# First modulation pieces as rows on TensorE, sums between the input transposes, and idle products in TensorE's waits

## What is computed

```python
c_act = silu(c)                                  # one row of 1,024
mod = c_act @ ada_w[layer] + ada_b[layer]        # 1,024 x 6,144 weights
sh_m, sc_m, g_m, sh_f, sc_f, g_f = split(mod, 6)
h = rms_norm(x, pre_mix_g) * (1 + sc_m) + sh_m   # the first normed input
u, v = split(gelu(h @ w_in + b_in), 2)           # the first large product
```

## Time and profile before

| | |
|---|---|
| median of 3 runs | 2,061.39 us (2,058.17 to 2,063.58) |
| the profiled execution's own time | 2,065.57 us |
| its span, first to last instruction | 2,063.9 us |
| mean granted TensorE clock | 0.980 |
| TensorE busy | 95% of the span |
| VectorE, ScalarE, GpSimd busy | 38%, 35%, 49% |

### The profile page before, as it was taken

How to read it: one execution, slowest core, us unless ns; L and a number is a source line. 1 busy time by engine, 2 the same in 40 slices (tenths; PEclk the granted TensorE clock), 3 DMA queues, 4 the chain that set the end, 5 groups by cost and what they waited for, 6 DMA issues and landing times. The chain is left out here.

```text
span 2063.9 us, 28068 instructions
## 1 busy us (share of the span) xinstructions
PE 1964.4 (95%) x10804; PEld 1680.5 (81%) x10804; DVE 792.3 (38%) x1382; ACT 717.5 (35%) x1153; POOL 1001.9 (49%) x541
## 2 busy tenths in 40 slices
PE   5999999999999989998998999999999999989997
PEld 5998888888888878877878888888777997857997
DVE  5666533444444046343634111010327750036212
ACT  2324325322221254343635222222534233335333
POOL 1635644466665434546633655544433443624642
PEclk9999999999999999999999999999999999998999
DMA  7655453556656313232112333322222334311232
GB/s 261 201 164 164 163 171 105 153 173 189 189 169 207 97 56 95 72 102 82 52 42 67 99 100 93 100 92 99 76 74 72 92 93 109 78 41 32 66 99 82
DMA packets 220323, 230.68 MB, mean 112 GB/s; under 512 B 15456, under 2 KB 185224, under 8 KB 219960
## 3 DMA queue, kind: packets, MB, share of 16 engines
q1 hardware_dynamic: 215392, 213.28, 34.3%
q10 hardware_dynamic: 4824, 15.88, 2.3%
HBM read 226.33 MB, written 2.79 MB: 111 GB/s over the span
## 5 line engine op out<-in xcount | busy, mean ns | idle before, releaser
L742 POOL TENSOR_TENSOR w_lo<-raw,w_hi 128x1024 fp32r<-128x1024 f32 (+1 forms) x296 | 732.2, 2488 | 577.8 <-ACT w_hi L735 577.6
L1391 PE MATMUL acc<-hh,w_hi 128*128 128x512 f32 (+1 forms) x1472 | 558.4, 379 | 18.8 <-DVE hl L2029 9.4
L1391 PE MATMUL acc<-hh,w_lo 128*128 128x512 f32 (+1 forms) x1472 | 549.5, 373 | 0.0
L1391 PE MATMUL acc<-hl,w_hi 128*128 128x512 f32 (+1 forms) x1472 | 549.2, 373 | 0.0
L735 ACT ACTIVATE w_hi<-raw 128x1024 fp32r<-128x1024 f32 (+1 forms) x296 | 308.3, 1051 | 396.8 <-DMA raw<-in_ffn_w_down 152.5
L1391 PEld LDWEIGHTS acc<-hh,w_hi 128*128 128x128 f32 x1472 | 280.8, 191 | 77.5 <-issue 17.4
L1391 PEld LDWEIGHTS acc<-hl,w_hi 128*128 128x128 f32 x1472 | 281.1, 191 | 48.1 <-issue 1.7
L1391 PEld LDWEIGHTS acc<-hh,w_lo 128*128 128x128 f32 x1472 | 280.5, 191 | 48.4
L1391 PE MATMUL acc<-w_hi,hh 128*128 128x256 f32 x704 | 203.3, 289 | 3.3 <-POOL hl L1272 3.3
L1391 PE MATMUL acc<-w_hi,hl 128*128 128x256 f32 x704 | 200.8, 285 | 0.0
L1391 PE MATMUL acc<-w_lo,hh 128*128 128x256 f32 x704 | 200.8, 285 | 0.0
(11 more groups left out here) (502 smaller groups left out, 2902.2 us busy)
## 6 DMA issues: line engine op xcount, KB each, us to landing
raw<-in_ffn_w_gu SPq DMA_DIRECT2D x176, 256.0 KB, 3.3
raw<-in_w_in SPq DMA_DIRECT2D x52, 512.0 KB, 3.6
ada_raw<-in_ada_w SPq DMA_DIRECT2D x50, 512.0 KB, 3.9
raw<-in_ffn_w_down SPq DMA_DIRECT2D x44, 512.0 KB, 3.6
raw<-in_a_w_in SPq DMA_DIRECT2D x32, 512.0 KB, 3.7
ada_raw<-in_ada_w ACTq DMA_DIRECT2D x30, 512.0 KB, 5.7
raw<-in_a_w_out SPq DMA_DIRECT2D x16, 512.0 KB, 3.6
ada_raw<-in_kv_ada_w SPq DMA_DIRECT2D x16, 512.0 KB, 5.4
```

Of the source, the lines that this page charges most:

```text
L742: eng.tensor_tensor(w_lo[:, s, part, :], raw[:, s, part, :], w_hi[:, s, part, :].bitcast(F32), ALU.subtract).then_inc(w_split, 1)
L1391: ins = pe.matmul(out, w, x, start=first and n == 0, stop=last and n == len(pairs) - 1, skip_group_check=check)
```

## The change

The first 2,048 modulation columns are cut into eight other pieces of 1 MB: 512 rows by 512 columns, named (column group, half of the rows). Three of them, (0,0), (0,1) and (1,0), go to TensorE, now with one column of `c_act` stationary and 512 columns of weights moving, so that the result is a row on one partition (`row_unit`); ScalarE copies the row, and `row_columns` turns it into four columns by products with a single one. The other five go to VectorE, four steps of 512 columns each, sums of one column group in one buffer; for (1,1) its sum joins TensorE's row. The sums over partitions move into the sequence of transposes: column group 2 ahead of the second row piece, group 1's row ahead of the third chunk, group 3 ahead of the sixth. Each VectorE step is followed by a drain. The inverse deviations and the diagonal follow the second VectorE piece and the parameter copies. Loads are in the new order, with VectorE's last piece between the first two weight units. ScalarE takes its root table ahead of the wait for `x` and splits the first two weight units after the first and second copy of `x`. Last, ten products of the identity with itself are issued at four points of TensorE's order: in both attentions between the first scores and the first transposes, in the last head's values ahead of its waits, and ahead of the waits before the sparse attention. Their result is read by nobody. Constants and semaphore numbers follow; the pieces' buffers and the wide columns' counts change by name only.

```diff
@@ -52,10 +52,12 @@
 KU = 4
 RING = 4
 REL_BUCKETS, REL_MAX_DIST = 32, 128
-ADA_PE = 2
+ADA_PE = ((0, 0), (0, 1), (1, 0))
+ADA_DVE = ((2, 0), (2, 1), (1, 1), (3, 0), (3, 1))
+ADA_HALF = 512
 ADA_SETUP = 8
-ADA_PAIRS = ADA_SETUP - 2
 ADA_WIDE = 1024
+WARM = 10
 ADA_WIDES = 12
 ADA_SLOTS = 48
...
@@ -582,6 +587,11 @@
             def last(n):
                 copy(n - 1)
             attention_loop(act, a, first, step, last)
+
+        def warm_products(pe, dst):
+
+            for _ in range(WARM):
+                pe.matmul(dst, ident[:], ident[:], start=True, stop=True)
 
...
@@ -626,6 +636,8 @@
                 pe.wait_ge(s, value)
             scores(0, 0)
             scores(0, 1)
+            pe.wait_ge(a["pt_dve"], 1)
+            warm_products(pe, aux[:, 0, 0:P])
             transposes(0)
...
@@ -765,22 +777,28 @@
         @block.sync
         def _(sp):
             sp.dma_start(c_row[:], io["c"][0].rearrange("(k p) -> k p", p=P)).then_inc(c_in, 16)
-            def whole_step(dst, s, landed_sem):
-                sp.dma_start(dst, ada_w[0][:, COLS * s:COLS * (s + 1)].rearrange("(k p) n -> p k n", p=P)).then_inc(landed_sem, 16)
-            def next_step(s):
-                whole_step(ada_next[:, s], ADA_PE + s, ada_next_in[s])
-            next_step(0)
-            whole_step(ada_first[:, 0], 0, ada_first_in[0])
-            next_step(1)
+            def ada_unit(dst, unit, landed_sem):
+                wide, half = unit
+                rows_k = ada_w[0][4 * P * half:4 * P * (half + 1), ADA_HALF * wide:ADA_HALF * (wide + 1)]
+                sp.dma_start(dst, rows_k.rearrange("(k p) n -> p k n", p=P)).then_inc(landed_sem, 16)
+            def pe_unit(s):
+                ada_unit(ada_unit_home(s), ADA_PE[s], ada_first_in[s])
+            def dve_unit(s):
+                ada_unit(ada_next[:, 1 + s], ADA_DVE[s], ada_next_in[s])
+            dve_unit(0)
+            pe_unit(0)
+            dve_unit(1)
             sp.dma_start(x_tok[:], io["x"][0].rearrange("(b p) d -> p b d", p=P)).then_inc(x_landed, 16)
-            for s in range(1, ADA_PE):
-                whole_step(ada_first[:, s], s, ada_first_in[s])
+            pe_unit(1)
             sp.wait_ge(x_landed, 16)
-            for s in range(2, ADA_SETUP - ADA_PE):
-                next_step(s)
-            load_group(sp, "mlp_v", 0, 0)
+            dve_unit(2)
+            pe_unit(2)
+            dve_unit(3)
+            load_unit(sp, S["mlp_v"], src_of["mlp_v"], 0, 0, 0)
+            dve_unit(4)
+            load_unit(sp, S["mlp_v"], src_of["mlp_v"], 0, 0, 1)
             load_group(sp, "mlp_v", 0, 1)
-            sp.wait_ge(ada_ready, ADA_SETUP - ADA_PAIRS)
+            sp.wait_ge(ada_setup_ready, 3)
...
@@ -993,14 +1011,19 @@
                     act.wait_ge(t_ready, c + 1)
                     act.activation(hi[:, k, :], tmp[:, c % 4, :], ACT.Copy).then_inc(h_hi, 1)
 
+            act.activation(warm[:], eps[:], ACT.Sqrt)
             act.wait_ge(x_landed, 16)
             for b in range(NB):
                 block_squares(b)
             act.activation(small[:, 0:NB], square_sum[:, 4, :], ACT.Sqrt, bias=eps[:], scale=1.0 / D).then_inc(std_ready, 1)
+            for wide, src in enumerate((ada_ps, bank(1))):
+                act.wait_ge(row_ps, wide + 1)
+                act.activation(ada_first[0:1, wide, 0, :], src[0:1, :], ACT.Copy).then_inc(row_sb, 1)
             for k in range(DC):
                 act.wait_ge(xt_ps, k + 1)
                 act.activation(x_first[:, k, :], XT_BANKS[k % len(XT_BANKS)], ACT.Copy).then_inc(kept_ready, 1)
-            split_hi(act, S["mlp_v"], 0, 0)
+                if k < 2:
+                    split_hi(act, S["mlp_v"], 0, 0, slice(k, k + 1))
...
@@ -1573,9 +1592,19 @@
                         wide_columns(slot // 4 - 1)
                 return before_chunk
 
-            def column_sums(dst, src):
-                for m in range(2):
-                    ins = pe.matmul(dst[:, m:m + 1], src[:, m * P:(m + 1) * P], ones[:, 0:1], start=True, stop=True)
+            def row_columns(wide):
+
+                pe.wait_ge(row_sb, wide + 1)
+                for m in range(4):
+                    pe.matmul(bank(0)[:, 4 * wide + m:4 * wide + m + 1], ada_first[0:1, wide, 0, m * P:(m + 1) * P], ones[0:1, 0:1],
+                              start=True, stop=True)
+
+            def setup_sums(wide, at):
+
+                pe.wait_ge(ada_setup_ready, at)
+                for m in range(4):
+                    ins = pe.matmul(bank(0)[:, 4 * wide + m:4 * wide + m + 1], ada_setup[:, wide - 1, m * P:(m + 1) * P], ones[:, 0:1],
+                                    start=True, stop=True)
                 return ins
...
@@ -1591,6 +1620,10 @@
                 for k in range(DC):
                     if k >= len(XT_BANKS):
                         pe.wait_ge(kept_ready, k - len(XT_BANKS) + 1)
+                    if k == 2:
+                        row_columns(1)
+                    if k == 5:
+                        setup_sums(3, 3).then_inc(ada_first_ps, 1)
                     for b in range(NB):
...
@@ -1602,23 +1635,27 @@
             pe.transpose(aux[:, 0, 0:DC], c_row[:], ident[0:DC, 0:DC]).then_inc(c_ps, 1)
 
             pe.wait_ge(c_ok, 1)
-            for s in range(ADA_PE):
+            def row_unit(s, dst):
+
+                wide, half = ADA_PE[s]
                 pe.wait_ge(ada_first_in[s], 16)
-                for m in range(2):
-                    for k in range(DC):
-                        pe.matmul(bank(0)[:, 2 * s + m:2 * s + m + 1], ada_first[:, s, k, m * P:(m + 1) * P], c_act[:, k:k + 1],
-                                  start=k == 0, stop=k == DC - 1)
+                for k in range(KU):
+                    ins = pe.matmul(dst, c_act[:, KU * half + k:KU * half + k + 1], ada_unit_home(s)[:, k, :],
+                                    start=half == 0 and k == 0, stop=half == 1 and k == KU - 1)
+                return ins
+
+            row_unit(0, ada_ps[0:1, :])
             pe.wait_ge(par_in, 16 * 19)
             for n, r in enumerate((112, 104, 74)):
                 pe.transpose(bank(1 + n)[:, 0:r], rows[0:r, n, :], ident[0:r, 0:r]).then_inc(par_t, 1)
+            setup_sums(2, 1)
+            row_unit(1, ada_ps[0:1, :]).then_inc(row_ps, 1)
             pe.wait_ge(par_ok, 3)
+            row_unit(2, bank(1)[0:1, :])
+            pe.wait_ge(ada_setup_ready, 2)
+            pe.matmul(bank(1)[0:1, :], ones[:, 0:1], ada_setup[:, 0, :], start=False, stop=True).then_inc(row_ps, 1)
+            row_columns(0)
             first_to_features()
-            for s in range(ADA_PE, ADA_PAIRS):
-                pe.wait_ge(ada_setup_ready, s - ADA_PE + 1)
-                ins = column_sums(bank(0)[:, 2 * s:2 * s + 2], ada_setup[:, s - ADA_PE, :])
-            ins.then_inc(ada_first_ps, 1)
-            for s in range(ADA_PAIRS, ADA_SETUP):
-                ada_column(s, s % 2)
...
@@ -1818,6 +1855,8 @@
 
             def head_values(h, e):
                 pe.wait_ge(m_s_ready, h + 2)
+                if h == MH - 1:
+                    warm_products(pe, ms[:, 0:P])
                 pe.wait_ge(hm_ready, h + 1)
...
@@ -1898,24 +1938,24 @@
 
             def wide_finish(q):
 
-                dve.wait_ge(ada_sum, ADA_SETUP - ADA_PAIRS + q + 1)
+                dve.wait_ge(ada_sum, q + 1)
                 cols = slice(2 * ADA_SETUP + DC * q, 2 * ADA_SETUP + DC * (q + 1))
                 dve.tensor_tensor(mod[:, cols], ada_ps[:, 0:DC], par_a[:, cols], ALU.add).then_inc(ada_col, 1)
 
-            def ada_chunks(total, w, k0):
-                for kk in range(w.shape[1]):
-                    if k0 + kk == 0:
-                        ins = dve.tensor_scalar(total, w[:, kk, :], c_act[:, 0:1], None, ALU.mult)
+            def ada_unit(n):
+
+                wide, half = ADA_DVE[n]
+                total = ada_setup[:, wide - 1, :]
+                dve.wait_ge(ada_next_in[n], 16)
+                for kk in range(KU):
+                    k = KU * half + kk
+                    if kk == 0 and (half == 0 or wide == 1):
+                        dve.tensor_scalar(total, ada_next[:, 1 + n, kk, :], c_act[:, k:k + 1], None, ALU.mult)
                     else:
-                        if kk:
-                            dve.drain()
-                        ins = dve.scalar_tensor_tensor(total, w[:, kk, :], c_act[:, k0 + kk:k0 + kk + 1], total, ALU.mult, ALU.add)
-                return ins
-
-            def ada_finish(step, par, summed):
-                dve.wait_ge(ada_sum, summed)
-                dve.tensor_tensor(mod[:, ds(2 * step, 2)], ada_ps[:, 2 * par:2 * par + 2], par_a[:, ds(2 * step, 2)], ALU.add) \
-                    .then_inc(ada_col, 1)
+                        dve.scalar_tensor_tensor(total, ada_next[:, 1 + n, kk, :], c_act[:, k:k + 1], total, ALU.mult, ALU.add)
+                    ins = dve.drain()
+                if half:
+                    ins.then_inc(ada_setup_ready, 1)
 
             def inverse_deviation(n):
```

(28 more changed lines are left out.)

26 lines of the change are left out of this document (13 added, 13 removed).

## The result

The changed kernel took 2050.97 us in the median of eight runs (2047.62 to 2055.25), the kernel before 2059.49 beside it (eight runs, 2055.44 to 2065.38). The ratio is 0.9949, 95% interval 0.9933 to 0.9965, so 10.5 us less (7.2 to 13.8). Two other points of scale: the profiled execution of the changed kernel took 2047.62 us (span 2045.9), at the low end of its runs, and the one of before 2065.57, at the top of its own. The profiled pair is thus 18.0 us apart in span, and this is more than the kernels are.

What follows compares the result with a forecast made beforehand. TensorE bounds the kernel, so only places where it stands still or runs at half clock pay: setup -5.0, attentions -4.5, -1.7, -0.4, -5.3, sum -16.9, from 2,061.4 to 2,044.5 us; range 2,037 to 2,054.

Steps and rivals of the forecast that it cites:

- first rival: Setup: row products do not raise the clock; first large product about 54.5, +1.6; 2,051.1 us in all; chance 0.15.
- fourth rival: Setup: splits between the copies hold ScalarE and the gain is given back; setup 0, 2,049.5 us; chance 0.06.
- I let it end at 39.9: Setup: VectorE's fifth piece, 36.5 undisturbed, ends at 39.9 because GpSimd's two weight splits run beside it.
- -6.5: Setup: the first large product starts at 46.4 in place of 52.90.
- -8.7: Setup, best case: clock also kept, so the half-clock stretch at the first large product's start shrinks, 2.2 more.
- -3.2: Setup, poor case: clock drops in the 2.5 us wait at 37.4; sums and three chunks cost 7.1, not 3.7.
- -5.0: Setup: the worth taken between the cases of -3.2 and -8.7.
- The first attention, -4.5: Idle products in the wait before the first transposes keep full clock to the third transposes; at most -4.8, floor 0.
- second rival: Attentions: idle products do not hold the clock, 1.2 to 1.9 us of wait remaining; 2,056.4 us; chance 0.12.
- The second attention, -1.7, -0.4 and -5.3: Idle products speed the last head's values (-1.7), the scores (-0.4) and first to third transposes (-5.3, at most -6.2).
- The base of the sum: -16.9 from the profiled 2,065.57 gives 2,048.7; that execution lies 4.2 above the median, so from 2,061.4: 2,044.5.
- third rival: Slower: clock never up before the x products and low where idle products are issued; 2,072 us; chance 0.05.

Runs made afterwards that it cites:

- columns_new_order: Changed kernel with TensorE's three setup pieces made as columns again, no one-row copies, same new order; ratio 0.9941 to the kernel before.
- fitted: Changed kernel with 16 idle products at the first attention, ten ahead of the first large product, 13, 8 and 11 at two norms and q projection; 0.9933.
- idle20: Changed kernel with 20 idle products in place of 10 in each of the three places; ratio 0.9971 to the kernel before.
- split_late: Changed kernel with the two first weight splits put after ScalarE's eight copies of x, as before; ratio 0.9966 to the kernel before.
- before_again: The kernel before, unchanged, run and profiled a second time; ratio 1.0005, profiled execution 2068.03 us.
- idle_first: Changed kernel keeping only the idle products ahead of the first transposes, in both attentions; ratio 0.9975, median 2056.28 us.
- idle_more: Changed kernel plus ten idle products in each of the setup's two waits, and more ahead of four norms and the q projection; ratio 0.9951.
- after_again: The changed kernel once more, unchanged, for a second trace and more timed rounds; ratio 0.9936 to the kernel before.

## Why the prediction was right, and where it was off

The forecast was 2,044.5 us, 16.9 less than before, in a range of 2,037 to 2,054; it came to 2,051.0, and to 10.5 less. The forecast's mechanism is the one that ran, at some 60% of its size. The time alone would not say so: 2,051.0 is also what the first rival gave (2,051.1), and the fourth lies at 2,049.5, both nearer than the forecast. It is the traces that rule these two out.

**Landings and pieces.** These terms hold to 0.4 us: x at 17.75 (17.8), the second row piece at 20.47 (20.6), VectorE's third, fourth and fifth pieces at 23.82, 28.59 and 32.81 (23.9, 28.9, 33.2). With 2 KB packets the queue moved 391, 389 and 388 GB/s in the windows of 2 us from 20 to 26 us, against 350 with 1 KB ones and the 380 that the forecast took.

**The row products and the clock.** The first rival fell: the pieces took 6.04 and 3.60 us, forecast 6.0 and 3.4, and in columns_new_order the one-column products stayed at half clock, 0.22 us a record from 20.56 to 34.2 us. That row products raise the clock "as well", from which the ends at 26.6 and 30.0 follow, was the author's assumption, resting on no run; and no run shows row pieces of 6.8 us each, half clock throughout, that give the first rival's end at 34.2: the longest, in fitted, took 6.57. The rows gave 0.43 us for a record of 512 columns at full clock (four span 1.88), 3.4 for eight and twice that at half clock, and for the one-column form 0.22 us at 10.44 and 0.115 at 41.35. The changed kernel showed 0.85 us from the start of one record of 512 columns to that of the next at half clock and 0.43 at full clock, and ends at 26.5 and 29.9. The first rise came 5.9 us into the x products in before (37.2), 5.2 into them in columns_new_order (41.1), and 2.8 to 5.7 us into the first row piece (12.4 in idle20, 15.2 in the changed kernel); the second row piece of the changed kernel had it 4.9 us from its start (25.4). What raises the clock no run showed.

**VectorE's last piece.** The term "I let it end at 39.9" is what happened in the commoner draw (32.7 + 7.1 to 7.2); in the other it ended at 38.0. split_late showed the cause, GpSimd's splits. The fourth rival fell: putting the splits late did not free the path but cost it, 48.66 in place of 44.6 or 48.1. The forecast's own sum to the first product, 46.4, was met by neither draw. In the one, the wait for the sums was 0.55 us and the clock was kept up to the product: 44.61, so -8.3 in place of -6.5 (the -8.7 had the clock kept behind the product as well, and there it fell). In the other, the 2.5 us wait it had named was 2.75 and the clock fell behind it: 48.07 to 48.17, so -4.8 where the forecast priced this case at -3.2. That the -5.0 taken between the cases lies so near the -4.8 of the commoner draw is in part luck, as both cases came out 1.6 to 1.8 us better than priced; timed, it is -3.7.

**The first attention, -4.5: the step that failed.** It took the full difference of 14.58 and a later pair, on the reasoning that ten idle products end inside the wait and hold the clock over "1.9 us of wait left". They held it in one execution of eight. By the means above the set is worth 2.1 us. The evidence used for it was one wait of 3.07 us that had kept the clock; this was one draw, and in the changed kernel's own profile the same wait of 3.07 us lost it. In the twelve profiled executions where nothing fills that wait, ten kept the clock and two lost it (after, before_again), while the 2.0 us left at the first attention lost it in seven of eight. So the length of a wait does not carry over from one place to another, and this is where the working had too little ground. So the second rival was right for this place, at 2.0 us left, and wrong for the other two, where 1.2 to 1.4 us are left and the clock was kept in each execution that had all three sets. Sixteen or twenty products at the first attention kept it in both cases tried.

**The second attention, -1.7, -0.4 and -5.3.** In the profiled pair these hold within 0.3 us: 1.7, 0.3 and 5.6. But their base was high: three executions without the sets lost 31.3, 26.7 and 27.9 us where the forecast knew only the first, and the average worth is 4.9 us in place of 7.4.

**The base of the sum.** The forecast set its own execution 4.2 us above the median and took that from the base, yet read every term from the same execution, as if its losses of the clock were every execution's. Lowering the base and keeping the terms counts the good luck of the median twice: an execution above the median is, on average, one that had more to win. This is argued and not shown; before_again lay 5.6 us above its median and had less to win in the two attentions (15.82 and 26.66 us, against 14.58 and 31.28), its losses lying elsewhere. With the averages above, -5.9 - 2.1 - 4.9 = -12.9, or -11.8 with the commoner setup, inside the measured 7.2 to 13.8.

**The third rival** (slower) did not come, but its second half was seen at work in idle_first, where the last scores and the first four of the set's twenty records ran at half clock (to 1857.8 us), so that the set started later and ran over, and the transposes came 1.4 to 1.6 us later. The clock that it kept behind them (10.35 us to the third transposes, against 11.48 and 15.97) made up for this: 27.00 in all, against a mean of 28.6 without any set.

What stays open: whether the setup's timed 3.7 us, below the 4.8 to 8.3 of the traces, is scatter or is partly returned later. Up to the first attention the commoner draw gives nothing back; behind it no run separated the two. Nor is it shown what lets the same wait keep the clock once and lose it the next time.

## What to carry to other kernels

A profile is one draw of the clock. Before pricing a stall that includes a clock loss, look at the same stall in every execution at hand and price its mean; do not lower the base by the profiled execution's bad luck while keeping terms read from it. Filling a wait with idle products paid here where what remained of it was short (first to third transposes in 9.80 and 9.81 us with 0.68 or nothing left, in 11.39 or 11.43 in seven of eight executions with 1.9 to 2.1 left), and it cost where the fill overran (26.74 us in idle20 against 23.7) or started late behind work at half clock (6.87 us from scores to transposes in idle_first against 5.23); size each fill to its own wait. When one engine's work slows another's, moving the disturbing work early can still be right, as the splits show (first large product at 44.6 or 48.1 with the piece at 5.2 or 7.1 us, at 48.66 with it at 3.23): what counts is which of its two places is on the path.

## What the runs showed of the hardware

- The granted clock fell or stayed behind the same wait from one execution to the next: the 3.07 us wait ahead of the q projection kept it in the first profile of before (1.00) and lost it in that of the changed kernel (half from 854.9 to 861.7 us). The mean clock of twelve timed executions of one kernel on one chip, before_again, ran from 0.975 (2070.06 us) to 0.985 (2053.57), and over the twelve it goes with the time at a correlation of -0.97: most of the scatter between its runs is the clock.
- The granted clock reads 1.00 up to the first change that a trace records, whatever the array does: up to 37.2 us in before, 15.2 in the changed kernel, 41.1 in columns_new_order (own reading of the clock records; each begins with a rise to 1.00). It is not a matter of the products' form. The window 12 to 15 us of the changed kernel reads 1.00 beside records of 512 columns that take 1.06 us each, as they do at a reading of 0.50 from 21 to 24 us, while those of the third piece, at a recorded 1.00, take 0.59; 20 to 34 us of columns_new_order reads 1.00 beside one-column records of 0.22 us, against 0.115 for the same form at 41.35. In the start, read the clock from the durations of single records. The mean clocks are too high by it, by some 0.009 in before, 0.004 in the changed kernel and 0.010 in columns_new_order (estimates: half of 37.2, 15.2 and 41.1 us over the span), so kernels with other setups are not compared by them.
- GpSimd's two weight splits of 2.5 us each stretched a VectorE piece of 3.23 us to 5.17 or to 7.1 us, with nothing between, in nine executions. It goes with where in the piece the splits began: 1.72 to 2.26 us behind its start (34.53 against 32.81) in the four of 5.2, 1.43 to 1.67 in the five of 7.1 to 7.3. Where the splits ran later, the piece took 3.23 us (split_late, and columns_new_order, where they began at 39.66). No run set this start by itself.
- With more idle products the mean clock was higher (0.989 in idle_more, 0.984 in after_again) without a measurable gain (medians of 2049.11 and 2049.94 us). The reading can be full while TensorE stands still, too: 1.00 from 860 to 865 us of before, with TensorE busy for 1.93 of the 5 us.
